# Later LayerNorm rows by block transposes, loads in finer groups, and another queue order in an 8-core encoder block

## The reference

```python
x   = layer_norm(x, ln_in)                       # 1: entry norm
u   = x @ w_in                                   # q | k | v | conv-GLU | branch gates: 3840 columns
y_a = windowed_gqa(q, k, v, bias, sink) @ w_attn_out   # keys within +-128 tokens, 16 blocks of 128
y_c = swish(LN(depthwise_conv31(glu))) @ w_conv_out
mix = (sigmoid(g_a) * y_a + sigmoid(g_c) * y_c) @ w_out
h   = layer_norm(ALPHA * x + mix, ln1_g, ln1_b)        # 2: uses the rows lnB1
x   = layer_norm(ALPHA * h + (silu(h @ w_gate) * (h @ w_up)) @ w_down, ln2_g, ln2_b)   # 3: uses the rows lnB2
```

## Time and profile before

| | |
|---|---|
| median of 3 runs | 911.23 us (906.44, 911.23, 915.03) |
| profiled execution | 907.42 us |
| its span on the slowest core (core 6) | 905.7 us |
| spans of the 8 cores | 892.9 to 905.7 us |
| TensorE (PE) busy on core 6 | 867.4 us, 96% |
| VectorE, ScalarE, GpSimd busy | 497.3, 276.9, 187.5 us |
| moved by DMA on core 6 | 94.22 MB, mean 104 GB/s |

### The profile page before, as it was taken

The page is one execution under the profiler, slowest core; times in us unless marked ns, Lnnn a source line. Parts: engine busy times, 40 slices in busy tenths (PEclk is TensorE's granted clock), DMA queues, the critical chain, the costliest instruction groups (busy, mean ns, idle before and its releaser), DMA issues.

```text
span 905.7 us, 16193 instructions; the slowest of 8 cores (892.9 to 905.7 us)
## 1 busy us (share of the span) xinstructions
PE 867.4 (96%) x5835; PEld 428.3 (47%) x5918; DVE 497.3 (55%) x713; ACT 276.9 (31%) x397; POOL 187.5 (21%) x267
## 2 busy tenths in 40 slices
PE   7899998979999999999999999999999999999996
PEld 5894453434444444443444444444444444444443
DVE  7894358868678662257143754543678312541254
ACT  4773267866664152211111011120001210011110
POOL 4220112212213233243311131211212202030000
PEclk9999999999999999999999999999999999999999
DMA  8969842660027415479983575684739806171101
GB/s 197 235 151 152 143 78 29 101 107 1 7 43 202 79 26 92 70 147 193 170 141 82 130 168 109 106 96 79 165 81 156 157 1 117 69 135 29 24 24 69
DMA packets 54349, 94.22 MB, mean 104 GB/s; under 512 B 16896, under 2 KB 23168, under 8 KB 54016
## 3 DMA queue, kind: packets, MB, share of 16 engines
q0 software_dynamic: 25488, 51.39, 36.0%
q1 hardware_dynamic: 28784, 41.81, 18.0%
HBM read 127.78 MB, written 13.63 MB: 156 GB/s over the span
## 4 chain that ended last, share of the span: by engine, by line
PE 82%; DMA 9%; DVE 4%; issue 3%; ACT 1%; POOL 0%; SPq 0%; DVEq 0%; POOLq 0%; ACTq 0%
PE ps L1387 29%; PE ps L935 17%; PE ps L1406 15%; PE ps L1267 6%; PE ps L1324 5%; PE ps L1010 3%; PE ps L1059 3%; DMA xt_54_96<-x 2%; DMA xE_143_185<-x 2%; DMA wco_130<-wco 1%; DMA wE_147_189<-wg 1%; PE ps L1218 1%; PE ps L1177 1%; DVE dw_38_80 L804 1%; DMA xE_141_183<-x 1%
## 5 line engine op out<-in xcount | busy, mean ns | idle before, releaser
L786 ACT ACTIVATE sgb_181_223<-ps 128x512 f32<-128x512 f32 x44 | 26.3, 597 | 178.8 <-PE ps L1387 98.6
L786 ACT ACTIVATE sgb_182_224<-ps 128x512 f32<-128x512 f32 x44 | 26.3, 597 | 172.9 <-PE ps L1387 96.8
L804 DVE TENSOR_TENSOR hid_222<-ps,sgb_182_224 128x512 bf16<-128x512 f32 x44 | 30.3, 689 | 84.5 <-PE ps L1387 81.2
L804 DVE TENSOR_TENSOR hid_222<-ps,sgb_181_223 128x512 bf16<-128x512 f32 x44 | 30.3, 689 | 82.5 <-PE ps L1387 82.5
L800 DVE SCALAR_TENSOR_TENSOR t_123_165<-gt_119_161,ps 128x512 f32<-128x512 f32 x16 | 10.9, 682 | 27.2 <-ACT gt_120_162 L786 22.2
L800 DVE SCALAR_TENSOR_TENSOR E_99_141<-ps,bias_100_142 128x1024 f32<-128x1024 f32 x15 | 18.3, 1220 | 10.7 <-PE ps L1177 10.7
L786 ACT ACT_TABLE_LOAD x12 | 15.4, 1283 | 24.8 <-DVE mv_18_60 L828 12.5
L800 DVE SCALAR_TENSOR_TENSOR t_125_167<-gt_121_163,ps 128x512 f32<-128x512 f32 x16 | 10.9, 680 | 21.2 <-ACT gt_122_164 L786 20.8
L800 DVE SCALAR_TENSOR_TENSOR E_97_139<-ps,bias_101_143 128x1024 f32<-128x1024 f32 x16 | 19.5, 1219 | 5.3 <-PE ps L1177 5.2
L800 DVE SCALAR_TENSOR_TENSOR xE_136_178<-xE_136_178,ps 128x512 f32<-128x512 f32 x8 | 5.5, 685 | 30.5 <-PE ps L1406 24.9
L1406 PE MATMUL ps<-wdn_179_221,hid_222 128*128 128x512 bf16 (+1 forms) x65 | 19.0, 372 | 1.6 <-DVE xE_142_184 L800 1.5
(11 more groups left out here) (785 smaller groups left out, 2072.3 us busy)
## 6 DMA issues: line engine op xcount, KB each, us to landing
xt_51_93<-x SPq DMA_DIRECT2D x4, 512.0 KB, 7.4
wE_149_191<-wg POOLq DMA_DIRECT2D x8, 256.0 KB, 7.2
wE_150_192<-wu POOLq DMA_DIRECT2D x8, 256.0 KB, 6.6
wE_145_187<-wg POOLq DMA_DIRECT2D x8, 256.0 KB, 6.0
wE_146_188<-wu POOLq DMA_DIRECT2D x8, 256.0 KB, 6.9
wE_147_189<-wg POOLq DMA_DIRECT2D x8, 256.0 KB, 6.4
wE_148_190<-wu POOLq DMA_DIRECT2D x8, 256.0 KB, 7.8
wout_173<-wout POOLq DMA_DIRECT2D x4, 512.0 KB, 9.6
```

The source lines that it names most:

```text
L786: sc.add("act", lambda e: e.activation(res(out), res(in_), func, **kw), reads=reads, writes=writes, cost=c, table=table, **k)
L804: sc.add(eng, lambda e: e.tensor_tensor(res(out), res(a), res(b), op), reads=reads, writes=writes, cost=dcost(n) if eng == "dve" else 0.1 ...
```

## The change

Two loads of 1 MB, `lnB1` and `lnB2`, go. In their place one 64 KB load (`lnv`) and four VectorE block transposes stand (`spread_row`, also used for `lnA`). `lnv` lies inside the buffer `junk` of the entry-norm statistics. The loads that shared the stage name `loadG` get names of their own (`bias0` to `bias2`, `loadAO`, `loadC`, `loadG0` to `loadG7`), as do the x reloads of `mix` (`xE<t>`), so each can have its own rank. In the planner, `MARGIN` comes from the table, transfers that end after 60 us count as later by `LATE` for the engine that uses them, and POOL's queue gets 1.2 shares of the wire to SP's 1. The whole table `RANK` is replaced (some 600 entries; a few are shown). Costs, matmuls, casts and stores are as before.

```diff
+    "#margin": 0.031, ("#late", "act"): 2.3575, ("#late", "dve"): 3.4795, ("#late", "pe"): 1.864,
...
+    "lnab1": 722.2501, "lnb0": 948.834, "lnb1": 126.8133, "lnc0": 538.9294, "lnc1": 1126.115, "lnv": 127.3541,
...
-    MARGIN = 0.3
+    MARGIN = RANK.get("#margin", 0.3)
+    LATE = {e: RANK.get(("#late", e), 0.0) for e in ("pe", "act", "dve")}
+    LATE_FROM = 60.0
+    SHARE = {"sp": 1.0, "pool": 1.2}
...
                 r = op.start if (op in s.order and op not in s.deps) else op.end + self.HOP
+                if op.dma and op.end > self.LATE_FROM:
+                    r += self.LATE.get(s.eng, 0.0)
...
-                heads = [v[0] for v in lines.values() if v]
+                heads = [(v[0], self.SHARE[q]) for q, v in lines.items() if v]
...
-                if live:
-                    nxt = min(nxt, clock[0] + min(h[1] for h in live) * len(live))
+                total = sum(w for _, w in live)
+                for h, w in live:
+                    nxt = min(nxt, clock[0] + h[1] * total / w)
...
+    lnv, _ = sb(RI + 20992, [128, 128], F32, "lnv")
...
+    def spread_row(dst, h, src, col, reg, regs):
+
+        lv = src[:, col:col + 32].rearrange("p (b o) -> p b o", o=1)
+        sc.add("dve", lambda e: e.transpose(dst[:, h * D:(h + 1) * D].rearrange("p (b o) -> p b o", o=32),
+                                            lv.to_broadcast([128, 32, 32])),
+               reads=[reg], writes=regs, cost=1.25)
...
     for j in (1, 2, 0):
+        stage("bias%d" % j, 350)
         load(biasb[j][:, :], bias_d[j], ["bias%d" % j])
+    stage("loadAO", 350)
...
+    stage("loadC", 350)
...
     for f in range(8):
+        stage("loadG%d" % f, 350)
...
-    load(lnB1[:, :], lnp_d[:, 0:2 * D], ["lnB1"], wire=3.25)
-    load(lnB2[:, :], lnp_d[:, 2 * D:4 * D], ["lnB2"], wire=2.7, rank=990)
+    stage("lnv", 500)
+    load(lnv[:, :], lnv_d, ["lnv"], wire=0.4)
+    for h in range(2):
+        stage("lnb%d" % h, 530)
+        spread_row(lnB1, h, lnv, 32 * h, "lnv", [("lnB1", h)])
+    for h in range(2):
+        stage("lnc%d" % h, 990)
+        spread_row(lnB2, h, lnv, 64 + 32 * h, "lnv", [("lnB2", h)])
...
+        was = sc.group, sc.cur
+        stage("xE%d" % t, sc.cur)
         load(xs[:, :], x_d[t * 128:(t + 1) * 128, :], xr)
+        sc.group, sc.cur = was
```

More of the change, by code:

```diff
@@ L38 @@
 RANK = {
[84 rows of a table removed]
-    ("loadO", "pool"): -40.07, ("loadO", "sp"): -432.38, ("loadQ", "pool"): 294.49, ("mix0", "act"): 46.08,
[14 rows of a table removed]
-    ("taps", "dve"): 6.81, ("wdn0", "pool"): -167.08, ("wdn10", "pool"): -314.99, ("wdn3", "pool"): 331.41,
[22 rows of a table removed]
-    "lnab1": 940.31, "loadA": 52.55, "loadG": 1399.56, "loadO": 77.62, "loadQ": 729.33, "mix0": 73.38, "mix1": 148.4,
[6 rows of a table removed]
+    "#margin": 0.031, ("#late", "act"): 2.3575, ("#late", "dve"): 3.4795, ("#late", "pe"): 1.864,
[95 rows of a table added]
+    ("lnb1", "dve"): -82.9561, ("loadA", "pool"): 127.0754, ("loadC", "pool"): 270.2103, ("loadG0", "pool"): 95.0236,
+    ("loadG5", "pool"): 147.0449, ("loadG6", "pool"): -11.2459, ("loadG7", "pool"): -256.0077,
+    ("loadO", "pool"): 32.1311, ("loadO", "sp"): -432.3838, ("mix0", "act"): 379.4602, ("mix0", "dve"): -186.9482,
[16 rows of a table added]
+    ("taps", "dve"): -32.8721, ("wdn1", "pool"): -44.7232, ("wdn10", "pool"): 367.9431, ("wdn3", "pool"): -469.6074,
[29 rows of a table added]
+    "loadA": -230.2135, "loadAO": 695.1633, "loadC": 1170.3678, "loadG0": -837.1447, "loadG1": 1657.576,
[11 rows of a table added]
 }
@@ L439, in transfer @@
                     return None
-                live = [h for h in heads if h[2] <= clock[0] + 1e-9]
-                nxt = min([h[2] for h in heads if h[2] > clock[0] + 1e-9], default=1e18)
-                if live:
-                    nxt = min(nxt, clock[0] + min(h[1] for h in live) * len(live))
+                live = [h for h in heads if h[0][2] <= clock[0] + 1e-9]
+                nxt = min([h[2] for h, _ in heads if h[2] > clock[0] + 1e-9], default=1e18)
+                total = sum(w for _, w in live)
+                for h, w in live:
+                    nxt = min(nxt, clock[0] + h[1] * total / w)
                 stop = min(nxt, lim)
-                for h in live:
-                    h[1] -= (stop - clock[0]) / len(live)
+                for h, w in live:
+                    h[1] -= (stop - clock[0]) * w / total
                 clock[0] = stop
@@ L630, in build @@
     x_d = din("x", [S, D])
-    lnp_d = din("lnp", [128, 4 * D])
+    lnv_d = din("lnv", [128, 128])
     win_d = din("win", [30, 128, 1024])
@@ L900, in build @@
     act(esink[:, 0:1], epsc[:, 0:1], AF.Exp, ["epsc"], ["esink"], n=1, src="sb", table=T_EXP)
+    def spread_row(dst, h, src, col, reg, regs):
[3 more added lines that the diff above has]
+               reads=[reg], writes=regs, cost=1.25)
     for h in range(2):
         stage("lnab%d" % h, -100)
-        lv = small[:, C_LN + 32 * h:C_LN + 32 * h + 32].rearrange("p (b o) -> p b o", o=1)
-        sc.add("dve", lambda e, h=h, lv=lv: e.transpose(lnA[:, h * D:(h + 1) * D].rearrange("p (b o) -> p b o", o=32),
-                                                        lv.to_broadcast([128, 32, 32])),
-               reads=["small"], writes=[("lnA", 2 * h), ("lnA", 2 * h + 1)], cost=1.3)
+        spread_row(lnA, h, small, C_LN + 32 * h, "small", [("lnA", 2 * h), ("lnA", 2 * h + 1)])
     stage("consts", 20)
@@ L1331, in mix @@
         ln_stats(xs, xr, mvs, rss, mk, rk, 4.0 * EPS, first=half)
-        ln_apply(xs[:, :], mvs[:, 0:1], rss, lnB1v[:, 0, :], lnB1v[:, 1, :], xs[:, :], xr, mk, rk, ["lnB1"], xr)
+        ln_apply(xs[:, :], mvs[:, 0:1], rss, lnB1v[:, 0, :], lnB1v[:, 1, :], xs[:, :], xr, mk, rk, [("lnB1", 0), ("lnB1", 1)], xr)
         hb = hbb[t % 2]
@@ L1442, in down @@
         if t < NT - 1:
-            ln_apply(xs[:, :], mvs[:, 0:1], rss, lnB2v[:, 0, :], lnB2v[:, 1, :], xs[:, :], xr, mk, rk, ["lnB2"], xr)
+            ln_apply(xs[:, :], mvs[:, 0:1], rss, lnB2v[:, 0, :], lnB2v[:, 1, :], xs[:, :], xr, mk, rk, [("lnB2", 0), ("lnB2", 1)], xr)
             store(xs, xr, 0, D)
             return
-        stt(xs[:, :], xs[:, :], mvs[:, 0:1], lnB2v[:, 0, :], ALU.subtract, ALU.mult, xr + [mk, "lnB2"], xr, n=1024)
+        stt(xs[:, :], xs[:, :], mvs[:, 0:1], lnB2v[:, 0, :], ALU.subtract, ALU.mult, xr + [mk, ("lnB2", 0)], xr, n=1024)
         for h in range(2):
             hs = slice(512 * h, 512 * h + 512)
-            stt(fin[:, hs], xs[:, hs], rss, lnB2v[:, 1, hs], ALU.mult, ALU.add, [xr[h], rk, "lnB2"], [("fin", h)])
+            stt(fin[:, hs], xs[:, hs], rss, lnB2v[:, 1, hs], ALU.mult, ALU.add, [xr[h], rk, ("lnB2", 1)], [("fin", h)])
             store(fin, [("fin", h)], 512 * h, 512 * h + 512)
@@ L1521, in prepare @@
     shared = {}
-    rep = lambda v: np.broadcast_to(f(v).reshape(1, -1), (128, f(v).size))
-    shared["lnp"] = np.ascontiguousarray(np.concatenate(
-        [rep(inputs["ln1_g"][0]), rep(inputs["ln1_b"][0]),
-         rep(inputs["ln2_g"][0]), rep(inputs["ln2_b"][0])], axis=1))
+    lnv = np.concatenate([f(inputs["ln1_g"][0]), f(inputs["ln1_b"][0]), f(inputs["ln2_g"][0]), f(inputs["ln2_b"][0])])
+    shared["lnv"] = np.ascontiguousarray(np.tile(lnv.reshape(128, 32).T, (4, 1)))
     pair = np.arange(512).reshape(2, 4, 64).transpose(1, 0, 2).reshape(512)
```

## The result

The change made the kernel 1.2% faster: median 900.25 us (899.01 to 901.34, 4 runs) against 910.8 us (4 runs), ratio 0.9884 with the interval 0.9835 to 0.9933. The profiled execution took 899.01 us, 897.4 us of it the span of its slowest core. Some executions run at a lower granted clock and take several per cent longer; all medians and ratios here leave them out.

What follows compares the result with a forecast made beforehand. TensorE, busy 867.4 of 905.7 us, bounds the kernel; only idle time can go. 907.4 - 2.1 (lnB2's load) - 4.8 (order) = 900.5, +1 for the median: 901 us predicted, range 892 to 913.

Steps and rivals of the forecast that it cites:

- Base and median: Whole kernel: sum starts from the profiled 907.4 us, 3.8 below the median; a quarter of that excess stays, +1 us.
- lnB2's load: SP near 400 us: removing this 1 MB load lets the transfers behind it land earlier, -2.1 us (bounds 0 and -2.2).
- lnB1's load: SP at 281 us: nothing waits for this 1 MB load, so removing it gives 0.
- the 64 KB load: SP, after the last entry-norm statistics: the new load is wanted 200 us later, so 0 (bounds 0 and +2).
- The four transposes: VectorE at 281 to 310 and 400 to 498 us: idle time covers their 5.0 us, so 0 (bounds 0 and +2.5).
- Finer groups and the other order: TensorE's remaining waits (wco, xE_142, wE_147, hid): planned slack covers late transfers, -4.8 us (bounds -10.7 and +6.4).
- three quarters of 6.4: Share of TensorE's remaining 6.4 us of waits on the late core that the new order removes, giving -4.8 us.
- rival D: All cores: the new order also shortens waits they share, a few us below 894.6, so 891 us; chance 0.05.
- rival B: Neighbouring cores: one stays late in any order, waits only move, just lnB2's 2.1 us gained, 909 us; chance 0.30.
- the bound of -10.7: Order's largest gain, if every core ran as the fastest does (905.7 to 892.9), lnB2's part taken off.
- What would show it: Expected in the profile after: TensorE idle and wco wait each under 1 us, spread some 6 us, fastest core near 893.
- Rival C: First w_conv_out matmul: the new order exposes up to 23.9 us of wco's covered delay, 923 us; chance 0.11.

Runs made afterwards that it cites:

- E1b: E1 with the two transposes of lnB1 some 20 us later on VectorE, just before the first mix product: 905.7 us, ratio 0.9975 to the kernel before.
- E1: The kernel before, order kept, only the two 1 MB loads replaced by the 64 KB load and four block transposes: 910.87 us, ratio 1.0016.
- E8: The kernel before, old ranks and loads, but its planner counts transfers ending after 60 us as late by LATE: 910.1 us, ratio 1.004.
- E3: The kernel after with chunk 1's four DMA transposes put between the h stores on SP: 899.0, 893.7 and 894.85 us in three sets.
- E5: The kernel after with 39 extra 256 KB copies within DRAM on SP, one each 20 us: 901.98 us, ratio 0.9927 to the kernel before.
- E4: The kernel before with 39 extra 256 KB copies within DRAM on SP, one each 20 us: 924.71 us, ratio 1.0164.

## Why the prediction was right, and where its steps were off

The forecast's time held (901 against 900.25 us; its sum, 900.5 and 1, is 901.5). Its mechanism, late transfers that a plan with slack no longer waits for, held in part. The larger part of the order's gain is one that it left out, so that the size fits so well is in part luck.

- *Base and median.* One us was kept for a median above its profile. The four runs after lie 0 to 2.3 us above the profiled one, the median 1.2. Right.
- *lnB2's load, -2.1.* E1b: -2.3, and the stretch named is the one that filled, on every core. The interval reaches to 0, so the size is borne out by the rows more than by the times.
- *lnB1's load, 0, and the 64 KB load, 0.* No wait shows either in E1b or after; the load lands 9.9 us after its issue at 73.9 us.
- *The four transposes, 0.* After, they take 1.23 to 1.25 us each, and from 262 to 310 us TensorE waits nowhere on seven cores and once, 1.1 us, on core 4, so the term held. Its working did not. "So 7.7 us of idle time cover 2.5" took a mean over 25 us for a place: at 281 us, the place that the prediction names, products stood in VectorE's queue that TensorE needed, and E1 paid 3.7 us for `lnB1`'s pair alone. The prediction had no cost for that pair, and its bound of 2.5 us was for `lnB2`'s. The planner put `lnB1`'s pair in front of such a product too, but gave TensorE something to do. Core 4 after, in order of time:

```profile
272.27 1.23 DVE L939 STREAM_TRANSPOSE lnB_136_178<-lnv_75 128x1024 f32<-128x1024 f32 x1
272.73 1.89 PE L974 MATMUL ps<-x0T_35_77,wG_116_158 128*128 128x512 bf16 x8
...
275.85 0.68 DVE L839 TENSOR_TENSOR Ob_96_138<-ps,den_29_71 128x512 bf16<-128x512 f32 x1
...
277.91 0.39 PE L1280 MATMUL ps<-ident_43,Ob_96_138 128*128 128x128 bf16 x4
```

  Here `Ob_96` comes late as well, but between 272.7 and 277.9 us three gate projections of 1.89 us stand on TensorE ahead of the matmul that uses it.
- *Finer groups and the other order, -4.8.* The size held, the make-up did not. From E1b to the kernel after the medians differ by 7.7 us. What the forecast has against it is the -4.8 and the 2.8 of the median's excess that it let go as lateness too, 7.6 together. Behind these numbers four things differ from "three quarters of 6.4":
  - The prediction put all idle time but the late cores' waits in front of the first and behind the last matmul, and so counted only waits that late cores have. But the attention waits lie in the middle and all cores share them: 3.9 us to 1.1 gave 2.8, a part of the fastest core's 5.2 us. By the spans of E1b and the kernel after, 4.6 of the slowest core's 7.6 us came off the fastest core too; where the rest of the 4.6 lies is not shown. I had that as rival D, at 0.05, because "it sees little more than it saw"; E8 shows that the new sight with the old ranks gains nothing, so the gain needs more than that.
  - What a late core gained beyond that is some 3 us. For `wco` the slack did grow, by 2.4 us, as the prediction has it ("2 to 3.5 us of slack").
  - The wait is not the whole price: the clock granted after it took another 1.7 us.
  - Against these, the new order put in a wait of its own (`wE_147`), with the same price in clock (0.94 over 30 us is 1.8 us), which the prediction named only as rival B's kind; E3 prices it at 3.2 us. Without it the term would be -10.9, just past the bound of -10.7.
- *What would show it.* The 1 MB loads, the transposes, 400 to 425 us and `wco` came as written. The spread went to 9.7 and not 6, and to 9.9 to 12.5 in the other three executions: the `gu` wait kept it; with E3's edit it is 6.2 (4.6 to 8.0 in the executions of its last two sets). The fastest core did not stay near 893: it gained 5.2 us.
- *Rival B, the waits move.* Partly: one did, and it was found and removed. As a law it fell: E5 loses about 3 us where E4 loses 14.9. The Trainium skill (HBM Reference, Specifications (TRN2)) says that the two cores of a domain share its bandwidth. From that the prediction took it that the partner makes the lateness. One core of each neighbouring pair is still the longer in the profiled execution after, by 3.8 to 7.5 us, which one changes between executions, and no run shows who the partners are. The 909 us that the prediction hung on that did not come (the prediction calls this rival the second; it is the first in its list): an order can leave lateness in place and not wait for it.
- *Rival C, the cover of `wco` goes.* The opposite came: POOL's issue stood 18.4 us earlier, still after a wait of 12.81 us, and the time from the issue to the place of the first use grew from 9.9 to 12.3 us.

What stays open: how the order's 7.7 us divide among the clock, the transfer waits and the shared waits, and what makes one neighbour late.

## What to carry to other kernels

Judge an order by what it loses when transfers are late: add known traffic to both and compare, since a quiet profile shows only the waits that happened. For one transfer, read the distance from its issue to its first use: for `wco` it grew from 9.9 to 12.3 us, though issue and use both moved by more than 16. To place an instruction, look at what is queued behind it at that moment and who waits for that, not at the engine's mean idle time in the stretch. After a replanning, look for bunches that the plan made by chance (here four DMA transposes in a row): undoing one was worth 3.2 us, the two removed transfers 2.3.

## What was not expected of the hardware

- Four DMA transposes issued in a row: issue on SP takes 7.0 us in the median and up to 10.7, where the two that E3's edit sets apart took 2.0 and 1.3. The four weight loads of 256 KB issued beside them landed after 16.9 to 21.4 us, the seven ahead of them after 4.1 to 8.6:

```profile
L995 SPq DMA_TRANSPOSE mT_129_171<-h_scratch x4: 1582/6970/10714, 449.5 to 469.7; - x4
```

- Waits of 3.9 and 3.2 us were followed by a lower granted clock: 0.95 over 35 us before, 0.94 over 30 us after. Both times it is some 4 us at 0.50 to 0.70, close to the 1.2 GHz level, which costs 1.7 to 1.8 us more. Where the wait was missing the clock was 1.00 (core 4 after in the first stretch, E3 in the second).
- Which core of a neighbouring pair is the longer one changes between executions: core 0 by 10.5 us in one set of the kernel after, core 1 by 4.2 in another.
